# A hybrid decoder trunk on one core: the stores of the expert outputs issued by ScalarE instead of GpSimd

## The reference

```python
logits = xf @ w_router                        # 512 tokens, 8 experts
top_vals, top_idx = lax.top_k(logits, 2)
gates = softmax(top_vals)
h = jax.nn.silu(xblk @ w1[e]) * (xblk @ w3[e])   # the tokens of expert e
y = h @ w2[e]
out[token] += gate * y                        # two rows per token
```

## Time and profile before

| | before |
|---|---|
| median of three executions | 2222.48 us (2221.13 to 2222.88) |
| the profiled execution, its own time | 2224.46 us |
| span in the profile | 2222.8 us |
| TensorE matmul busy | 2070.9 us, 93% of the span |
| VectorE busy | 1536.5 us, 69% |
| ScalarE busy | 1197.4 us, 54% |
| GpSimd busy | 84.3 us, 4% |
| share of TensorE in the chain that ended last | 87% |
| mean DMA rate | 220 GB/s |
| mean granted TensorE clock | 0.974 of full speed |

### The profile page before, as it was taken

One profiled execution on the slowest core, in us unless ns is written; L12 is line 12 of the kernel. 1 busy time (PEld: TensorE's weight loads), 2 busy tenths in 40 slices (PEclk: granted clock), 3 DMA queues, 4 the chain that ended last, 5 costly groups with the idle time before them and its releaser, 6 DMA issues.

```text
span 2222.8 us, 30246 instructions
## 1 busy us (share of the span) xinstructions
PE 2070.9 (93%) x9627; PEld 1708.7 (77%) x9628; DVE 1536.5 (69%) x1667; ACT 1197.4 (54%) x1493; POOL 84.3 (4%) x122
## 2 busy tenths in 40 slices
PE   5989999999979996999999999999999998999991
PEld 4767788888867775888788878787888787878881
DVE  6885666666667856665666688896666897876655
ACT  4442555555544423554555577776555776765543
POOL 1000000000000003000000000000000000000002
PEclk9999999999989997999999999999999999999996
DMA  7221866656632214666666699998665999996643
GB/s 228 91 66 38 289 187 187 186 185 189 189 123 95 76 57 143 227 226 208 235 225 221 215 370 374 334 379 307 226 226 196 364 373 331 374 333 226 227 151 128
DMA packets 245647, 489.64 MB, mean 220 GB/s; under 512 B 16564, under 2 KB 86308, under 8 KB 245604
## 3 DMA queue, kind: packets, MB, share of 16 engines
q1 hardware_dynamic: 236288, 461.43, 60.5%
q0 software_dynamic: 7936, 27.03, 3.7%
q10 hardware_dynamic: 1380, 0.61, 0.1%
HBM read 473.80 MB, written 15.22 MB: 220 GB/s over the span
## 4 chain that ended last, share of the span: by engine, by line
PE 87%; DVE 5%; issue 3%; DMA 2%; ACT 1%; POOL 0%; ACTq 0%; DVEq 0%; POOLq 0%
PE PS L1168 85%; PE PS L1419 1%; DMA raw<-in_expert_w 1%; DVE wlo L598 1%; DVE PS L670 1%; PE PS L1185 1%; ACT whi L327 1%; PE PS L1422 1%; DVE OV L631 1%; DMA OV<-in_norm_mix_g 0%; DVE XN L615 0%; POOL SM L1019 0%; DVE OV L794 0%; DMA raw<-y_rows,addr 0%; ACT XN L345 0%
## 5 line engine op out<-in xcount | busy, mean ns | idle before, releaser
L1168 PE MATMUL PS<-whi,XN 128*128 128x512 f32 x3616 | 1125.3, 394 | 9.6 <-DVE XN L807 4.9
L598 DVE TENSOR_TENSOR wlo<-raw,whi 128x1024 fp32r<-128x1024 f32 x882 | 1035.2, 1220 | 138.7 <-ACT whi L327 132.7
L327 ACT ACTIVATE whi<-raw 128x1024 fp32r<-128x1024 f32 x882 | 885.4, 1052 | 106.3 <-DMA raw<-in_expert_w 50.3
L1168 PEld LDWEIGHTS PS<-whi,XN 128*128 128x128 f32 x3616 | 682.6, 189 | 156.3 <-issue 15.5
L1168 PE MATMUL PS<-wlo,XN 128*128 128x512 f32 x2144 | 773.0, 391 | 0.0
L1168 PE MATMUL PS<-XN,whi 128*128 128x512 f32 x1408 | 478.7, 400 | 5.2 <-DVE XN L615 4.7
L1168 PEld LDWEIGHTS PS<-wlo,XN 128*128 128x128 f32 x2144 | 404.9, 189 | 82.9
L1168 PE MATMUL PS<-XN,wlo 128*128 128x256 f32 (+1 forms) x1088 | 341.5, 314 | 0.0
L1168 PEld LDWEIGHTS PS<-XN,whi 128*128 128x128 f32 x1408 | 266.4, 189 | 72.1 <-issue 6.4
L1168 PEld LDWEIGHTS PS<-XN,wlo 128*128 128x128 f32 x1088 | 206.1, 189 | 15.0
L491 ACT ACTIVATE XN<-PS 128x512 fp32r<-128x512 f32 x56 | 33.5, 598 | 192.1 <-PE PS L1422 151.7
(11 more groups left out here) (195 smaller groups left out, 1030.6 us busy)
## 6 DMA issues: line engine op xcount, KB each, us to landing
raw<-in_expert_w SPq DMA_DIRECT2D x672, 512.0 KB, 5.2
raw<-in_ffn_w SPq DMA_DIRECT2D x144, 512.0 KB, 3.7
raw<-in_w_in SPq DMA_DIRECT2D x40, 512.0 KB, 4.7
raw<-in_w_out SPq DMA_DIRECT2D x16, 512.0 KB, 4.2
y_rows<-OV POOLq DMA_DIRECT2D x8, 512.0 KB, 5.3
y_rows<-OV POOLq DMA_DIRECT2D x1, 3072.0 KB, 11.6
RES<-in_x SPq DMA_DIRECT2D x4, 512.0 KB, 5.3
x_tok<-OV POOLq DMA_DIRECT2D x4, 512.0 KB, 2.9
```

What stands on the lines that cost most here:

```text
L327: act.activation(whi[:, u0 % CONV, half(h)], raw[:, r, half(h)], ACT.Copy).then_inc(s["hi_done"], 1)
L598: dve.tensor_tensor(wlo[:, w, half(h)], raw[:, u0 % RAW, half(h)], whi[:, w, half(h)].bitcast(F32), ALU.subtract).then_inc(s["lo_done"], 1)
L1168: return pe.matmul(out_, lhsT, rhs, start=start, stop=stop, skip_group_check=True)
```

## The change

The two stores of each visit leave GpSimd's program. ScalarE issues them on its own queue, right after it has copied the output to `yt` and before `x_split_ext`. Since the rows in `yt` are complete only when both its own copy and VectorE's addition have landed, ScalarE first waits for `y_evac`. GpSimd still waits for `y_stored` between its gathers. The 3 MB store of zeros moves too: ScalarE issues it between the two halves of layer 0's dense mixer, where GpSimd did it near the start of that mixer. The 1.5 MB store of zeros stays where it was. In the new program the lines stand one higher from line 151 on, and up to nine higher in GpSimd's part.

```diff
--- before.py
+++ after.py
@@ -148,6 +148,7 @@
         y_rows = nc.dram_tensor("y_rows", [VIS * WIN, D], F32)
         l_rows = nc.dram_tensor("l_rows", [WIN * VIS, 1], U32)
 
+        y_v = y_rows[:, :].rearrange("(s v) n -> s v n", v=VIS)
         names = """x0 x1 x2 x3 raw00 raw01 raw10 raw11 raw20 raw21 prm_in bd_in gB0_in gB_in gF_in rw_in
           const_ok bd_zero step prm_T prm_ok lam_exp sp_ok rw_hi rw_ok warm_up
           ss_done mean_done rs_done xt_done xT_done xhi_done xlo_done x_stored
@@ -530,6 +531,10 @@
                     act.sem_inc(s["y_part"], 1)
                 act.activation(yt[:, 0, :].rearrange("p (a n) -> p a n", a=2), PS[:, 4:6, :],
                                ACT.Copy).then_inc(s["y_evac"], 1)
+                act.wait_ge(s["y_evac"], i * 2 + 6)
+                for n, (a, b) in enumerate(((0, P), (P, WIN))):
+                    act.dma_start(y_v[a:b, bass.ds(i, 1), :].rearrange("s v n -> s (v n)"),
+                                  yt[0:b - a, n, :]).then_inc(s["y_stored"], 16)
                 x_split_ext(i + 1)
                 m_split(i, g, 9, 10)
 
@@ -561,6 +566,10 @@
 
                     act.activation(warm, mhalf, ACT.Silu).then_inc(s["warm_up"], 1)
                     for h in range(2):
+                        if h:
+                            act.wait_ge(s["list_zero"], 1)
+                            act.dma_start(y_v[0:P, E:VIS, :],
+                                          gath[:, 0:1, :].broadcast_to([P, VIS - E, D])).then_inc(s["y_stored"], 16)
                         with act.Fori(0, FFN_G // 2) as g:
                             hidden(FFN_BASE + 3 + h * 3 * FFN_G, g * 6, g * 2, F0 + h * 2 * FFN_G, g * 4, HALF)
             act.wait_ge(s["gd_ok"], 1)
@@ -1066,11 +1075,9 @@
             pool.wait_ge(s["w1_done"], F0 + 1)
             pool.memset(gath[:, 0, :], 0.0).then_inc(s["list_zero"], 1)
             pool.wait_ge(s["list_zero"], 1)
-            y_v = y_rows[:, :].rearrange("(s v) n -> s v n", v=VIS)
             l_v = l_rows[:, :].rearrange("(s v) one -> s (v one)", v=VIS)
             blocks = ((0, P), (P, WIN))
             zeros = gath[:, 0:1, :].broadcast_to([P, VIS - E, D])
-            pool.dma_start(y_v[0:P, E:VIS, :], zeros).then_inc(s["y_stored"], 16)
             pool.dma_start(y_v[P:WIN, E:VIS, :], zeros[0:WIN - P]).then_inc(s["list_out"], 16)
             for a, b in blocks:
                 pool.dma_start(l_v[a:b, :], gath[0:b - a, 0, 0:VIS].bitcast(U32)).then_inc(s["list_out"], 16)
@@ -1123,10 +1130,6 @@
             def visit(i):
 
                 gather(i + 1)
-                held(s["y_evac"], i * 2 + 6)
-                for n, (a, b) in enumerate(blocks):
-                    pool.dma_start(y_v[a:b, bass.ds(i, 1), :].rearrange("s v n -> s (v n)"),
-                                   yt[0:b - a, n, :]).then_inc(s["y_stored"], 16)
                 held(s["y_stored"], i * 32 + 48)
                 held(s["gath_in"], i * 32 + 64)
 
```

## The result

| | before | after |
|---|---|---|
| median of five executions of each | 2222.48 us (2220.02 to 2223.88) | 2232.67 us (2232.15 to 2234.25) |
| ratio after to before, 95% interval | | 1.0046 [1.0035, 1.0058] |
| the profiled execution: own time, span | 2224.46, 2222.8 us | 2234.25, 2232.5 us |
| GpSimd busy | 84.3 us | 74.4 us |
| mean granted TensorE clock | 0.974 | 0.969 |

The changed kernel is slower by 10.2 us, 0.46%: twice the 5.0 us forecast, and inside the range. GpSimd's seventeen DMAs and 9.9 us of its busy time are gone, and nothing came of it.

What follows compares the result with a forecast made beforehand. The prediction took TensorE and the path between visits to bound the kernel, GpSimd's work being worth nothing. Its terms, 1.3 + 0.6 + 1.3 + 1.4 + 0.4, sum to 5.0 us more, predicting 2227.5 us, range 2220.5 to 2234 us.

Steps and rivals of the forecast that it cites:

- The bound: TensorE holds 87% of the chain, GpSimd 0%; only the path from one visit into the next counts.
- The stall d: ScalarE between output copy and `XE`: wait, two issues and register steps delay `XE` 1.3 us, 1.1 without an extension.
- into visit 1: TensorE reaches its extension matmuls just as `XE` is ready, without slack, so it is late by 1.3 us.
- into visits 2 and 5, the waits: TensorE waits for a late weight load; 1.3 less 0.65 for the earlier store, about 0.7 each, 1.4 us.
- into visits 3 and 6, the waits: The decisive weight half queues behind others; issued 1.1 us later it queues less, 0.2 us each leaks, 0.4 us.
- into visits 4 and 7, `XE`: VectorE was busy with splits and takes up part of the delay; 0.3 us each, 0.6 us.
- after the last visit: The last gather waits for VectorE behind ScalarE's unused weight splits, so the whole delay arrives: 1.3 us.
- The clock: Rival, slower still (0.14 with other cases): longer TensorE waits into visits 2 and 5 lower its clock, some 2 us each, 2231.5 us.
- Absorbed: Rival (chance 0.27): splits and queues take up the delay except into visit 1 and after the last visit; 2.2 us, 2224.7 us.
- Faster: Rival (0.11): weights get through sooner at four boundaries into visits without an extension; 4.6 us less, 2217.9 us.
- The gather goes ahead: Rival, slower still (0.14 with other cases): GpSimd's gather precedes needed loads, 1.95 us at four boundaries; 12.8 us, 2235.3 us.
- does not do what it says: Rival (no chance of its own): ScalarE's stores run through GpSimd's queue, leaving only the delay at the boundaries it reaches.

Runs made afterwards that it cites:

- wait_issues: Kernel before, GpSimd still storing; ScalarE also waits for `y_evac` and issues two small spare transfers before `x_split_ext`: 2235.09 us, 1.0057.
- after_xsplit: The change with the wait and two stores moved behind `x_split_ext`, ahead of the splits of weights: 2227.35 us, 1.0018 to the kernel before.
- four_issues: The change with each visit store cut into halves, four issues for the same bytes: 2249.26 us, 1.0127 to the kernel before.
- visits_only: Only the visit stores move to ScalarE, both stores of zeros stay with GpSimd: 2232.67 us, 1.0041 to the kernel before.
- issues_only: Kernel before, GpSimd still storing; ScalarE also issues two small spare transfers after each output copy, without waiting for `y_evac`: 2223.21 us, 1.0006.
- xe_first: Against the kernel before: ScalarE makes `XE` high, copies the output, splits four weight halves, then waits and stores: 2223.06 us, 1.0002.
- after_splits: The change with the wait and two stores moved behind `x_split_ext` and the four splits of weights: 2220.39 us, 0.9991 to the kernel before.
- evac_last_pool: Kernel before, GpSimd still storing; `XE` and the weight splits come before the output copy and VectorE's addition: 2222.47 us, 1.0002.
- evac_last_act: The change with `XE` and the weight splits before the output copy, ScalarE storing right behind that copy: 2239.50 us, 1.0080 to the kernel before.

## Why the prediction was half right

**The bound, right.** GpSimd's work was worth nothing, and the path at the boundaries was all. The store of zeros, put at nothing, is at 1.0000.

**The stall d, right in kind and too small.** The prediction gave the pair of issues 0.82 us and the register steps 0.15 us. Measured from VectorE's addition, which ended at 1068.24, `XE` starts 1.41 us later and not 0.97. So d is 1.71 us where 1.3 stood, and above its upper bound of 1.6; without the extension 1.42 where 1.1 stood. Taken issue by issue, the two took 0.392 and 0.593 us, 0.985 together where 0.82 stood. The remaining 0.43 us lies around them, where four register steps of 0.037 us, 0.15 us, stood. The short steps themselves are five of 0.029 to 0.037 us, 0.17 us together; the rest is time between one instruction and the next. Into visit 3 it is 0.88 us of issues and 0.42 us around them. So the step that failed is above all the 0.15 us: it counted the steps and not the time between them. Taking the smaller store at SyncE's median, 0.373, was the second miss, since it is the dearer of the two; that the first was put too high, at 0.448, made up for part of it. That the issues would overlap arithmetic if their wait were met, the prediction didn't see either; its working stands nonetheless, since in the change the wait is never met in time.

**The boundaries, term by term.**

| term | forecast | measured | from |
|---|---|---|---|
| into visit 1 | 1.3 | 1.8 | new wait of 1.58 us, table of events |
| into visits 2 and 5, the waits | 1.4 | 1.6 | 3.35 less 2.65, 3.62 less 2.73 |
| into visits 3 and 6, the waits | 0.4 | 0.4 | 5.22 less 4.82, 4.91 less 4.95 |
| into visits 4 and 7, `XE` | 0.6 | 1.3 | 0.6 (1.51 less 0.89) and 0.7 (6.39 at 2003.28 less 5.68) |
| after the last visit | 1.3 | 2.6 | 10.68 less 8.04 |
| lower or higher clock after the waits | 0 | 3.4 | +3.3 in visits 2 and 5, -1.6 in 6, +1.7 in 7 |
| other, up to visit 0 and at the end | 0 | -1.3 | -0.36 and 9.7 less 10.68 |
| sum | 5.0 | 9.7 | the terms as rounded give 9.8 |

The leak of 0.7 us each into visits 2 and 5 was 0.70 and 0.89 us, but for another reason than the one given: with the store left on GpSimd (`wait_issues`) it was 0.68 and 0.69, so the 0.65 us taken off for the earlier store is not borne out, and the figure was luck. Into visits 4 and 7 the prediction's own numbers, `XE` split at 1525.3 and wanted at 1525.07, give 0.2 us each and not 0.3. The waits into visits 3 and 6 match only in their sum. The late load into visit 3 did queue less, as argued: it landed in 7.38 us against 8.06. This is that load in the chain after:

```profile
1403.88 7.38 DMA raw<-in_expert_w
```

The stall itself thus came to 7.7 us against 5.0. The term after the last visit is the one most out: one issue there took 1.592 us. Issues as long are in the traces of `after_xsplit` (1.697 us), `wait_issues` (1.373) and `four_issues` (1.261), but not in that of `visits_only` (at most 0.598), which has the change's stores and was as slow. So the long issue isn't what the loss hangs on. The traces show what went on beside it. From 2189.21 to 2190.41 us a 16 KB packet of queue q8, which carries instructions, was under way, and the long issue began at 2189.22. This is the queue between 2189.2 and 2190.4 us:

```profile
q8 instruction: 1, 0.02, 6.3%
```

In each of the four traces the long issue, the second of its visit, began while such a packet was under way and ended 0.4 to 0.7 us after it. But two others that began beside one took 0.36 and 0.37 us (in `issues_only` and `xe_first`). So the packet may be what held the long ones up; no run tests it.

**The clock, a rival that came partly true.** "The clock falls also into visits 2 and 5", some 2 us each and 2231.5 us in all, is what the trace shows, 1.6 to 1.7 us each, beside 1.7 us more in visit 7 and a gain in visit 6 that nobody forecast. By the prediction's own list it is wrong in this point: the clock did change in the groups after the waits. But the rival's reason, the longer wait, isn't borne out by the table of the clock.

**The other rivals.** *Absorbed* falls: every boundary but those into visits 3 and 6 passed d on at least in part. *Faster* falls: with the store on ScalarE's queue, out of GpSimd's, and no stall (`after_splits`), at most 0.2% is gained, and the landing into visit 3 fell to 7.38 us and not below 6.8. The rule of the Trainium skill, "DMA: Bandwidth & Descriptors", section "Issuing engines are not separate DMA queues", that another issuer saves only the time of initiating the DMA, agrees with this: moving the stores by itself gave nothing that can be told. *The gather goes ahead* isn't seen as a term; the waits into visits 3 and 6 grew by 0.40 and -0.04 us. That the change *does not do what it says* falls with q10's bytes.

## What to carry to other kernels

Before moving a DMA to a compute engine, ask whether the semaphore that it waits for is already counted up when the engine's queue comes to it. If it is, the issue is hidden behind arithmetic already begun; if it is the engine's newest result, the engine drains, waits and then pays each issue in full, at a place where the next engine is waiting. Put such a store behind the work that others need next. Price a stall from the start of one instruction to the start of the next, and not from the durations alone, and price each issue from one with as many rows. Look also at what else the queue did ahead, such as loads that decide a branch.

## What the runs showed of the hardware

- ScalarE's queue runs ahead of its arithmetic. With no unmet wait, two issues of 1.14 us together started 0.17 us into the ACTIVATE two places ahead of them (1065.28 against 1065.11), and cost 1.0006 [0.9997, 1.0015].
- The lead ends at an unmet wait of an earlier instruction: with the fourth half waiting for its load until 1399.46, the pair behind it was issued at 1399.68 (`after_splits`).
- The time of an issue on ScalarE's queue depended little on the bytes of a row: 128 rows of 4 KB and 128 rows of 512 bytes, each with its smaller second one, took 1.15 us for the pair. Fewer rows didn't make it shorter: 128 rows took 0.355 to 0.454 us, 64 rows 0.48 to 0.60 us, but for the long ones below. Four in a row took 3.36 us for the same bytes that two moved.
- A single issue took 1.26 to 1.70 us after the last visit in four traces, each time beginning while a 16 KB packet of instructions was under way (two others that did so took 0.37 us), against a median of 0.45, and no more than 0.6 us there in others with the same stores.
- ScalarE's load of one value from `sizes` took a median of 0.28 us in `evac_last_pool` and 0.89 us in `evac_last_act`. Why isn't shown.
- The granted clock after a wait of 2 to 3.9 us was 1.00 or 0.89, in no order of the wait's length; it is worth 1.6 us a visit here.
